# Down projections of two MLPs as seven block products instead of eight, with summed weight blocks kept in DRAM

## The reference, cut to what matters

```python
def squared_relu_mlp(u, w_up, w_down):
    return jnp.square(jax.nn.relu(u @ w_up)) @ w_down
...
        f = squared_relu_mlp(rmsnorm(h, norm_mlp_pre[i]), w_up[i], w_down[i])
        h = h + rmsnorm(f, norm_mlp_post[i])
```

## Time and profile before

| | |
|---|---|
| median of 3 runs | 1336.4 us (1336.34 to 1336.48) |
| span of the profiled execution, first to last instruction | 1335.1 us |
| PE busy | 1324.6 us (99%) |
| DVE busy | 687.9 us (52%) |
| ACT busy | 588.6 us (44%) |
| POOL busy | 114.5 us (9%) |
| DMA, read and written | 133.41 MB and 2.93 MB, 102 GB/s over the span |

### The profile page before, as it was taken

How to read it: one execution, slowest core, us unless ns; L and a number is a source line. 1 busy time by engine, 2 the same in 40 slices (tenths; PEclk the granted TensorE clock), 3 DMA queues, 4 the chain that set the end, 5 groups by cost and what they waited for, 6 DMA issues and landing times.

```text
span 1335.1 us, 18387 instructions
## 1 busy us (share of the span) xinstructions
PE 1324.6 (99%) x6935; PEld 1093.5 (82%) x6935; DVE 687.9 (52%) x1080; ACT 588.6 (44%) x1105; POOL 114.5 (9%) x131
## 2 busy tenths in 40 slices
PE   9999999999999999999999999999999999999998
PEld 7778888888788888888888898777898888888886
DVE  5586677887436443223443364875474432244333
ACT  6645455676435443213332344765354322133321
POOL 0044352660000000000000000000000000000000
PEclk9999999999999999999999999999999999999999
DMA  7343433243432323233222233112223323322221
GB/s 221 104 126 100 130 103 102 93 163 112 159 109 80 99 93 108 95 127 95 94 98 92 79 100 119 48 64 80 79 81 102 114 98 110 95 94 95 97 100 72
DMA packets 75551, 137.75 MB, mean 103 GB/s; under 512 B 6342, under 2 KB 16854, under 8 KB 75478
## 3 DMA queue, kind: packets, MB, share of 16 engines
q1 hardware_dynamic: 71184, 134.76, 31.2%
q10 hardware_dynamic: 4294, 2.00, 0.8%
HBM read 133.41 MB, written 2.93 MB: 102 GB/s over the span
## 4 chain that ended last, share of the span: by engine, by line
PE 97%; DVE 1%; DMA 1%; ACT 1%; issue 1%; DVEq 0%; ACTq 0%
PE G L1733 64%; PE X L1733 12%; PE X L1756 7%; PE G L1806 3%; PE X L1806 3%; PE X L1912 1%; PE X L1921 1%; PE X L1995 1%; PE X L2210 1%; PE X L2182 1%; PE X L2200 1%; DMA raw<-in_w_mem_kv 1%; PE X L1934 1%; PE X L1974 1%; PE X L1983 0%
## 5 line engine op out<-in xcount | busy, mean ns | idle before, releaser
L1118 DVE TENSOR_TENSOR wlo<-raw,whi 128x1024 fp32r<-128x1024 f32 x207 | 252.6, 1226 | 441.9 <-ACT whi L567 440.8
L567 ACT ACTIVATE whi<-raw 128x1024 fp32r<-128x1024 f32 x207 | 217.7, 1058 | 421.3 <-PE G L1733 209.7
L1733 PE MATMUL G<-uhi,whi 128*128 128x512 f32 x736 | 294.3, 400 | 0.2 <-DVE ulo L1135 0.2
L1733 PE MATMUL G<-uhi,wlo 128*128 128x512 f32 x736 | 287.1, 390 | 0.0
L1733 PE MATMUL G<-ulo,whi 128*128 128x512 f32 x736 | 286.7, 390 | 0.0
L1733 PEld LDWEIGHTS G<-uhi,whi 128*128 128x128 f32 x736 | 138.2, 188 | 31.2 <-issue 1.1
L1733 PEld LDWEIGHTS G<-uhi,wlo 128*128 128x128 f32 x736 | 138.1, 188 | 29.5 <-DVE wlo L1166 0.2
L1733 PEld LDWEIGHTS G<-ulo,whi 128*128 128x128 f32 x736 | 138.3, 188 | 28.4
L1733 PE MATMUL G<-whi,hidhi 128*128 128x512 f32 x256 | 99.6, 389 | 0.0
L1733 PE MATMUL G<-whi,hidlo 128*128 128x512 f32 x256 | 99.6, 389 | 0.0
L1733 PE MATMUL G<-wlo,hidhi 128*128 128x512 f32 x256 | 99.6, 389 | 0.0
(11 more groups left out here) (342 smaller groups left out, 2240.5 us busy)
## 6 DMA issues: line engine op xcount, KB each, us to landing
raw<-in_w_up SPq DMA_DIRECT2D x64, 512.0 KB, 3.8
raw<-in_w_down SPq DMA_DIRECT2D x64, 512.0 KB, 3.5
raw<-in_ssd_w_in SPq DMA_DIRECT2D x20, 512.0 KB, 3.6
raw<-in_w_mem_kv SPq DMA_DIRECT2D x16, 512.0 KB, 3.6
raw<-in_ssd_w_out SPq DMA_DIRECT2D x16, 512.0 KB, 3.5
raw<-in_swa_w_in SPq DMA_DIRECT2D x16, 512.0 KB, 3.8
raw<-in_ssd_w_in SPq DMA_DIRECT2D x16, 384.0 KB, 3.4
csrow<-cs_rows SPq DMA_DIRECT2D x16, 384.0 KB, 4.4
```

Source lines behind the costliest of these rows:

```text
L567: act.activation(whi[q][:, :, :], raw[q % 2][:, :, :], ACT.Copy).then_inc(hi_done, 1)
L1118: dve.tensor_tensor(wlo[q][:, :, :], raw[q % 2][:, :, :], whi[q][:, :, :].bitcast(F32), ALU.subtract).then_inc(lo_done, 1)
L1733: mm = pe.matmul(o, st, mv, start=(kt == 0 and fresh and not go_on), stop=(q == total - 1 and k == 1), skip_group_check=True)
```

## The change

The down projection of each MLP is cut into 2 x 2 x 2 blocks (256 tokens, 2048 hidden rows, 512 output columns) and done as seven block products M1 to M7 (the Winograd form of Strassen's method) in the order M5, M2, M3, M1, M4, M7, M6.

- **PE.** Each product has 8 panels, and a panel now serves two token tiles: 12 matmuls. M3 and M4 go on in the banks of M5 and M2, M7 in those of M1. M6 is the last: its last four panels are done tile by tile, with `turn_u` between.
- **Weights.** Three products take blocks of `w_down` as they are. Four take sums of blocks, which lie in DRAM as `tsum`, four blocks of 4 MB for each layer. GpSimd issues the transfers that make them, of 1 MB each: 16 copies during SSD units 0 to 7 (both layers), then for each layer 24 (16 adding ones, 8 copies), each at a panel listed in `W0_SUM_AT` or `W1_SUM_AT`. SP waits for `sum_in` ahead of each product that uses a sum, and has four `raw` buffers during the products.
- **Left operand.** The relu and square now leave full float32 values `hid`; the eight up blocks follow each other. High and low parts are made for each product anew, in 28 chunks of `[128, 4, 256]` (`left_parts`), and the differences of left blocks in place by DVE, 16 chunks (`left_sums`).
- **Outputs.** `w_sum`, `e_sum`, `o1` and `o0` hold partial results. The second half of each token tile is now completed by an addition on DVE (`late_half`), and `norm_out` reads its result and no longer PSUM. Tiles 0 and 1 are complete when M7 is, and their `norm_out`, `gained` and `add_out` stand inside M6.
- The start of `split` has fewer steps on ACT and DVE (no parts are made there).

```diff
+M5, M2, M3, M1, M4, M7, M6 = range(PROD)
+LEFT = ((0, 0), (1, 0), (0, 1), (0, 1), (1, 1), (0, 0), (1, 0))
+PARTS_AT = {(M5, 0): (M5, 2), (M5, 1): (M5, 3)}
+PARTS_AT |= {(r, 2 * c + 2): (r + 1, c) for r in range(PROD - 1) for c in range(3)}
+PARTS_AT |= {(r + 1, 0): (r + 1, 3) for r in range(PROD - 1)}
+SUMS_AT = {(M5, 1): (1, 3), (M2, 3): (2, 0), (M2, 5): (2, 1), (M2, 7): (2, 2), (M3, 1): (2, 3),
+           (M3, 5): (4, 0), (M3, 7): (4, 1), (M1, 3): (4, 2), (M1, 5): (4, 3),
+           (M4, 3): (3, 0), (M4, 7): (3, 1), (M7, 3): (3, 2), (M7, 5): (3, 3)}
+WEIGHT_SUM = {M2: (0, (5, 11)), M1: (2, (8, 14)), M7: (1, (6, 12)), M6: (3, (10, 16))}
+W0_SUM_AT = tuple(range(54, 64)) + tuple(range(72, 100, 2))
+W1_SUM_AT = tuple(range(162, 184, 2)) + tuple(range(190, 216, 2))
...
+                for r in range(PROD):
+                    if r in WEIGHT_SUM:
+                        for x in range(4):
+                            sp.wait_ge(sum_in[x], 16 * WEIGHT_SUM[r][1][i])
+                    for q in range(8):
+                        n = 8 * r + q
+                        sp.wait_ge(lo_done, P_DOWN[i] + n - (1 if n < 2 else 3))
+                        sp.dma_start(down_raw[n % 4][:, :, :], right(i, r, q)).then_inc(down_in[n % 4], 16)
...
+            def weight_add(i, x, f, j, r, done):
+
+                rows = slice(512 * r, 512 * r + 512)
+                src = a["w_down"][i][2048 * f:2048 * f + 2048, 512 * j:512 * j + 512][rows, :]
+                ps.wait_ge(sum_in[r], 16 * done)
+                ps.dma_start(tsum[i][x][rows, :], src, accum_op=ALU.add).then_inc(sum_in[r], 16)
...
             for v in range(UNITS):
                 g, c = divmod(v, NT)
                 gh = slice(SR * g, SR * g + SR)
+                if v < 8:
+                    for r in range(2 * (v % 2), 2 * (v % 2) + 2):
+                        weight_copy(v // 4, v // 2 % 2, r, v // 2)
...
+            for i, at_panel in enumerate((W0_SUM_AT, W1_SUM_AT)):
+                for n in range(24):
+                    ps.wait_ge(panel_done, at_panel[n])
+                    weight_sum(i, n)
...
+                def right_hi(n):
+
+                    act.wait_ge(down_in[n % 4], 16 * (DOWN * i + n // 4) + 16)
+                    act.wait_ge(panel_done, P_DOWN[i] + n - 3)
+                    act.activation(whi[n % 4][:, :, :], down_raw[n % 4][:, :, :], ACT.Copy).then_inc(hi_done, 1)
...
+            def late_half(i, t):
+
+                product_ready(dve, i, M7 if t < 2 else M6, t % 2)
+                bank, part = (X[t], w_sum[:, t, :]) if t < 2 else (X[t], e_sum[:, t - 2, :])
+                dve.wait_ge(w_full if t < 2 else e_full, 2 * i + t % 2 + 1)
+                dve.tensor_tensor(halves(t)[1], bank[:, :], part, ALU.add).then_inc(late_done, 1)
+
             def boundary(m, nb):
 
-                gained(m, 0)
-                add_out(m, 0)
-                scaled(m, 0)
-                gained(m, 1)
-                add_out(m, 1)
+                if m % 2 == 0:
+                    gained(m, 0)
+                    add_out(m, 0)
+                    scaled(m, 0)
+                    gained(m, 1)
+                    add_out(m, 1)
                 scaled(m, 1)
-                gained(m, 2)
-                u_lo(m, 0)
+                if m % 2:
+                    u_lo(m, 0)
+                    late_half(m // 2, 2)
+                    gained(m, 2)
+                else:
+                    gained(m, 2)
+                    u_lo(m, 0)
                 lo(nb, 0)
                 u_lo(m, 1)
                 add_out(m, 2)
                 lo(nb, 1)
+                if m % 2:
+                    late_half(m // 2, 3)
                 gained(m, 3)
...
+                for r in range(PROD):
+                    for q in range(8):
+                        if r == M6 and q < 2:
+                            late_half(i, q)
+                        if (r, q) in SUMS_AT:
+                            left_sums(*SUMS_AT[r, q])
+                        if 8 * r + q + LOOK < 8 * PROD:
+                            right_lo(8 * r + q + LOOK)
+                        if (r, q) in PARTS_AT:
+                            left_parts(*PARTS_AT[r, q])
...
+                        elif (r, q) in ((M6, 1), (M6, 2)):
+                            gained(m, q - 1)
+                            add_out(m, q - 1)
+                            if i == 0 and q == 2:
+                                scaled(m, 0)
...
+                def product(r, panels):
+
+                    for q in range(panels):
+                        operands(r, q)
+                        mm = block_product(r, 0, q)
+                        if q == 7:
+                            mm.then_inc(prod_tile0, 1)
+                        block_product(r, 1, q).then_inc(panel_done, 1)
```

More of the change, by code:

```diff
@@ L360, in load @@
             def load(src, blk, q):
-                if not (isinstance(blk, int) and 4 * blk + q < 2):
+                if isinstance(blk, int) and blk == B_KV and q < 2:
+                    sp.wait_ge(lo_done, 4 * blk + q - 3)
+                elif not (isinstance(blk, int) and 4 * blk + q < 2):
                     sp.wait_ge(lo_done, 4 * blk + q - 1)
@@ new lines, in mlp, with left_parts @@
+                for f in range(2):
+                    with act.Fori(1 - f, 4 - f) as j:
+                        ahead(blk + 4 * f + j, skip=DOWN * i)
+                        squares(f, j)
+                def right_hi(n):
+                    act.wait_ge(down_in[n % 4], 16 * (DOWN * i + n // 4) + 16)
+                    act.wait_ge(panel_done, P_DOWN[i] + n - 3)
+                    act.activation(whi[n % 4][:, :, :], down_raw[n % 4][:, :, :], ACT.Copy).then_inc(hi_done, 1)
+                def left_parts(r, c):
+                    if r in SUM_OF:
+                        act.wait_ge(left_sum, 16 * i + 4 * SUM_RANK[SUM_OF[r]] + c + 1)
+                    else:
+                        act.wait_ge(hidsq_done, 36 * i + (20 if r < M3 else 36))
+                    if (r, c) not in ((M5, 0), (M5, 1)) and r < M6:
+                        act.wait_ge(panel_done, P_DOWN[i] + max(8 * r + 2 * c - 6, 0))
+                    act.activation(left(r, c)[0], chunk_of(LEFT[r], c), ACT.Copy).then_inc(left_hi_done, 1)
@@ L1090, in _ @@
             mlp(1, F_F1, B_F1)
-            for t in range(NT):
+            for t in range(2, NT):
                 norm_out(3, t)
@@ new lines, in right_lo, with left_parts @@
+                def right_lo(n):
+                    dve.wait_ge(hi_done, P_DOWN[i] + n + 1)
+                    dve.tensor_tensor(wlo[n % 4][:, :, :], down_raw[n % 4][:, :, :], whi[n % 4][:, :, :].bitcast(F32),
+                                      ALU.subtract).then_inc(lo_done, 1)
+                def left_parts(r, c):
+                    hi_at, lo_at = left(r, c)
+                    dve.wait_ge(left_hi_done, 28 * i + 4 * r + c + 1)
+                    dve.tensor_tensor(lo_at, chunk_of(LEFT[r], c), hi_at.bitcast(F32),
+                                      ALU.subtract).then_inc(left_lo_done, 1)
@@ L1701, in _ @@
             mlp(1, F_F1, B_F1)
-            for t in range(NT):
+            for t in range(2, NT):
+                late_half(1, t)
                 gained(3, t)
@@ new lines, in mlp, with block_product @@
+                with pe.Fori(1, UP) as j:
+                    gemm(N_F[i] + j, blk + j, 4, weights_still(u_of), u_wait(U0[2 * i + 2]), bank(f0 + j))
+                def block_product(r, t, q):
+                    hi_at, lo_at = left(r, q // 2)
+                    rows, o = slice(P * t, P * t + P), BANKS[r][t][:, :]
+                    s, fresh = q % 4, r not in (M3, M4, M7)
+                    for k in range(2):
+                        kt = 2 * (q % 2) + k
+                        pe.matmul(o, hi_at[:, kt, rows], whi[s][:, k, :], start=(fresh and q == 0 and k == 0),
+                                  stop=False, skip_group_check=True)
+                        pe.matmul(o, lo_at[:, kt, rows], whi[s][:, k, :], start=False, stop=False,
+                                  skip_group_check=True)
+                        mm = pe.matmul(o, hi_at[:, kt, rows], wlo[s][:, k, :], start=False,
+                                       stop=(q == 7 and k == 1), skip_group_check=True)
+                    return mm
@@ new lines, in mlp @@
+                for x in range(2):
+                    pe.wait_ge(bank_free[x], f0 + UP)
+                product(M5, 8)
+                for x in range(2, 4):
+                    pe.wait_ge(bank_free[x], f0 + UP)
+                product(M2, 8)
+                pe.wait_ge(m5_kept, 2 * i + 2)
+                product(M3, 8)
+                pe.wait_ge(half_free, 4 * i + 4)
+                product(M1, 8)
+                pe.wait_ge(w_done, 2 * i + 2)
+                product(M4, 8)
+                pe.wait_ge(e_full, 2 * i + 2)
@@ new lines, in mlp @@
+                product(M7, 8)
+                pe.wait_ge(ulo_ready, U0[2 * i + 2] + 8)
+                product(M6, 4)
```

(14 more changed lines are left out.)

376 lines of the change are left out of this document (237 added, 139 removed).

## The result

The changed kernel takes 1315.9 us (median of 4 runs, 1314.58 to 1320.05); the kernel before took 1336.4 us beside it. The ratio is 0.985, with a 95% interval of 0.983 to 0.986. The gain is 20.5 us, where 39.4 were forecast. The sign was right. The time lies outside the range of 1293 to 1311.

The account below looks back on a forecast made before the run. PE, busy 99%, was taken as the bound. Removed matmuls -43.5, M6 +0.9, boundary +1.8, tail +0.65, SSD part +0.3, sum transfers +0.5 gave -39.4 us: 1336.4 to 1297.0 us, range 1293 to 1311.

Parts of the forecast that it names:

- The transfers that make the sums: 64 DRAM transfers of 1 MB beside the panel loads: 0.5 us lost, bounds 0 and 25.
- I take 5 us for an adding one.: Time of a 1 MB adding transfer, taken between 2.5 and 14 us; it then fits an up block's free 7.4 us.
- 62 us of work meet 54 us.: Panels 54 to 63: sum transfers plus panel loads exceed the time, leaving 8 us of backlog for the next eight panels.
- Here too 8.3 us are allowed, with three panels in hand.: Panel loads beside the sum transfers may land up to 8.3 us after issue, against 3.5 us plus some expected.
- second rival: Sum transfers of 8 us or more crowd out panel loads from panel 54 and in up blocks: 1304 to 1321 us, chance 0.14.
- fourth rival: Late sums make SP hold back loads, perhaps through a DVE lock on GpSimd's descriptors; slower than before, about 1375 us, chance 0.05.
- Removed work: Down projections of both layers: 192 matmuls less on PE, 1344 in place of 1536, saving 43.5 us.
- Products M5 to M7: Block products of the down projection: DVE, 84 to 91% busy, keeps PE's pace; 0 us lost.
- M6: Last product, its last four panels done tile by tile: 0.7 us lost in layer 0, 0.2 in layer 1.
- Boundary: Behind layer 0's MLP, PE waits 1.05 us for wlo and 0.7 for u_tok: 1.8 us, bounds 0.9 and 3.5.
- Tail: Kernel's end: DVE adds between the last matmul and ACT's start; 0.65 us lost, bounds 0.6 and 1.0.
- third rival: DVE becomes the bound in some four of seven products, 8 to 20 us lost: 1304 to 1316 us, chance 0.11.

Follow-up runs that it names:

- e1: Changed kernel without any transfer that makes a sum; the four products that use sums read plain blocks of w_down instead: 1295.6 us.
- experiment 3: Changed kernel with the eight adding transfers of panels 54 to 61 turned into plain copies of the same size: 1299.2 us.
- experiment 4: Changed kernel with the four loads of h issued behind the load of panel 61 instead of panel 59: 1306.8 us.
- e7: e2 with layer 1's transfers of panels 180 and 182 moved into layer 1's up blocks: 1300.1 us.
- e9: e1 with tile 2's norm and the next panel's halves ahead of tile 3's late half behind layer 0's MLP: 1293.4 us.
- experiments 10 to 12: Low halves made twice on DVE: every second panel, 1325.8 us, every panel, 1383.7 (both on e2 plus boundary reorder and e7's edit); every second on e9, 1312.6.
- e2: Changed kernel with layer 0's ten transfers of panels 54 to 63 moved, so that ten run in the first six products: 1301.1 us.

## Why the prediction was wrong

The step that failed is the term **"The transfers that make the sums", 0.5 us**, of which the runs show 20.3 (e1). The mechanism of PE's bound was right; this term was mis-sized, in three steps:

- *"I take 5 us for an adding one."* It took 6.6 us of all engines (experiment 3), a copy 2.8 to 3.2 where 2.5 was taken. The copies out of `tsum` landed after 5.7 us and the adding ones after 10.1 (medians). The page "DMA: Bandwidth & Descriptors" of the Trainium skill, section "Anatomy of one DMA", has a formula for a transfer that GpSimd issues. It gives 4.4 us for 1 MB (an estimate from that page), which the trace does not bear out here: the fastest copy landed after 5.0 us, the fastest adding one after 8.8.
- *"62 us of work meet 54 us."* With 6.6 us it is 8 x 6.6 + 2 x 2.8 + 17 = 75 us. The 7.5 us for `h` and the gains, whose load showed at a share of 1.03 in this very stretch, were not in the sum. That makes 83 us in 54: a backlog of 29, not 8, as much as the next eight panels leave free.
- *"Here too 8.3 us are allowed, with three panels in hand."* This took each load to be issued in time. SP's queue had `h` and the gains ahead of panel 60's load, and it landed after 21 us (experiment 4).

The 8 us which the second rival asked for were too high a threshold, because they came from the same sum. The rival itself, with 1304 to 1321 us and a chance of 0.14, is what happened: in the stretch that it named, through `whi` waiting for DMA. Its estimate of many small losses was not what happened: 16.4 of 20.3 us came in one stage, in two waits with the slow clock behind them.

The transfers also cost 1.9 us in the second mixer (e7), 1.5 at the boundary (3.6 there in all against 2.1 in e1) and 0.4 in the SSD part, where 0.3 was taken. The last is less than that part scatters: the first marks of kernels that lose nothing behind it lie between 433.83 and 437.06. GpSimd's issues took 0.67 us for a copy in the SSD part, as "0.6 to 1" had it, and 1.0 for an adding one later.

The fourth rival did not come. SP waits for no sum in the changed kernel, and no issue of an adding transfer takes over 1.12 us, so the lock that it names shows nowhere in this trace.

**Right, with sizes.** *Removed work, 43.5 us*: e9 shows 331.10 us between marks, to 0.01 us the 352.86 of before less 21.76. *Products M5 to M7, 0*: right in e1 and e9. *M6, 0.7 and 0.2*: 0 in both layers (e9). *Boundary, 1.8 us, with 1.05 us for `wlo` and 0.7 for `u_tok`*: 2.1 without transfers, with 1.3 and 0.4 waited. The working holds in its main step. In the changed kernel the late half of tile 3, ACT's square and the gain come in the order in which they were summed (DVE in order of time):

```profile
771.22 0.68 DVE L1642 TENSOR_TENSOR e_sum<-X,e_sum 128x512 f32<-128x512 f32 x1
772.70 0.69 DVE L1590 TENSOR_TENSOR e_sum<-e_sum,g_post 128x512 f32<-128x512 f32 x1 [0.79 <-ACT junk L1004]
...
775.34 1.23 DVE L1275 TENSOR_TENSOR wlo<-raw,whi 128x1024 fp32r<-128x1024 f32 x1 [0.43 <-ACT whi L693]
```

From the addition to the multiplication lie 1.48 us, where the earlier trace rows had the multiplication 1.14 us behind `wlo` with nothing between. *Tail, 0.65*: 0.7. DVE does its addition of 0.69 us ahead of ACT's square:

```profile
1308.37 0.69 DVE L1642 TENSOR_TENSOR e_sum<-X,e_sum 128x512 f32<-128x512 f32 x1 [1.74 <-PE X L2392]
```

**DVE.** "84 to 91% busy" in the products was somewhat high. 31.74, 34.45 and 31.11 us of 40 in e9 are 78 to 86%. The third rival, that DVE bounds the products, is refuted for this kernel. But the forecast gave no margin, and experiments 10 to 12 show that it is small: at 17.5 us of work a product of 21.76 has room for three more operations of 1.22 us, and four more in each product cost 19 us even without transfers.

## What to carry to other kernels

Price a transfer that adds by the share of the DMA engines it takes, not by its bytes, and add up everything that runs in the same stretch, each queue's other loads too. Work that has slack should be released by what it may not collide with (a `split`, a boundary, loads of a state), since a panel count is not a clock. And the same few buffers cover late loads and a late engine only once: measure the margin with both present. When a run misses a sum of work by much, count the operations in the stretch again before looking for a new mechanism.

## What was not expected of the hardware

- Adding into DRAM takes 2.0 to 2.4 times a copy's share of the engines (6.6 us for 1 MB against 3.2 for copies mostly of the same source and 2.8 for copies out of `tsum`), at nearly the same GB/s (214 against 195).
- After PE had stood still from 360 us on, the granted clock was 0.50 at 365 to 370 us and 0.75 at 370 to 375, though PE was back at work at 368.73. Of the 16.4 us lost in that stage, 12.7 are waits in the list; such slow stretches are where the other 3.7 can lie.
- DMA engines at a share of 0.9 to 1.0 for 120 us cost PE nothing in the products, with four buffers and a panel wanted every 2.72 us (e2), while in the output projection, with two buffers and a shared queue, a share of 1.08 made PE stop.
